# First layer of a four-stage decoder kernel: the input norm's scale is applied behind the projections instead of ahead of them

## The chip, the cores and the metric

One program runs on one core of a Trainium2 chip. The metric is device time in microseconds of one execution, from inputs in HBM to the output in HBM, as the median of several runs. Everything is in float32; products are made of parts, since a 32-bit value is split into a high part that TensorE takes in its fast 32-bit format and a low part with what is left.

TensorE (PE) multiplies, VectorE (DVE), ScalarE (ACT) and GpSimd (POOL) work on rows, SyncE (SP) issues most DMAs. Each engine runs its own list of instructions in order; semaphores connect them.

## The reference

The reference runs three blocks with 256 tokens of width 1024; only the first layer of the first block is touched. In it:

```python
def rmsnorm(x, g):
    xf = x.astype(jnp.float32)
    y = xf * lax.rsqrt(jnp.mean(xf * xf, axis=-1, keepdims=True) + EPS)
    return (y * g.astype(jnp.float32)).astype(x.dtype)

hn = rmsnorm(x, even_norm[i])
proj = hn @ even_w_in[i]
q, k, v, u = jnp.split(proj, [SWA_WIDTH, SWA_WIDTH + KV_WIDTH, SWA_WIDTH + 2 * KV_WIDTH], axis=-1)
q = rmsnorm(q.reshape(b, l, SWA_Q_HEADS, HEAD_DIM), q_norm[i])
k = rmsnorm(k.reshape(b, l, SWA_KV_HEADS, HEAD_DIM), k_norm[i])
v = v.reshape(b, l, SWA_KV_HEADS, HEAD_DIM)
o_attn = swa_sink_attention(q, k, v, sinks[i])
o_ssm = s5_mixer(u, ssm_a_re[i], ssm_a_im[i], ...)
mixed = jnp.concatenate([o_attn, o_ssm], axis=-1) @ even_w_out[i]
```

A factor that belongs to a token can be applied to `x` or, since the product is linear, to `proj`. For q and k a second norm per head follows, `q * rsqrt(mean(q*q) + EPS)`: with unscaled products q' and the token's scale s it is `q' * s * rsqrt(s*s*mean(q'*q') + EPS)`. `s5_mixer` is a state space model: it takes exponentials, sines and cosines of small parameter tables (a few instructions on 128x16 values), builds powers and matrices from them on DVE, and scans over the tokens.

## The kernel before

**Strips.** Every weight matrix is cut into strips of 128x1024 values, listed in the order of use (`strip_names`): in the first layer ("even") k, q0 to q3, v, u0 to u3 are strips 0 to 9, then follow parts of the output matrix and of the gate. A ring of three buffers holds them. SP issues strip n when strip n - 3 has its low part (`low_ready`, L499 and L500). ACT makes the high part (`high(n)`, L1254, which also waits until PE has done strip n - 3), DVE (`low(n)` in its own list, L1762) or POOL (`low(n)`, L2620) the low part. `high_to(n)` makes all high parts up to n that are still to be made.

**The first norm** (i = 0). ACT squares and sums each half of the tokens and takes the root (L1290, L1291), DVE inverts it and writes a diagonal matrix with the scales (`scale_diag`, L1807, L1808), PE multiplies x by this diagonal, which turns x and scales it (L687), and ACT (`parts`, L1280) and DVE (`parts`, L1798) write the high and the low part of `hT`, the normed and turned input, from PSUM. Between the roots and its `parts`, ACT makes high(0), two exponentials and two sines of the state space tables (L1303 to L1308); DVE makes low(0) and `decay_angles` (L1826 to L1844), which the sines wait for in the middle. POOL clears four areas, waits for the diagonals, and clears a fifth, `e_X` (L2632).

In the later layers the norm is taken differently (`SCALED_OUT` = [1, 2, 3]): x is turned as it is (`turn_x`, L665), PE spreads the scales over all rows (`widen_scale`, L673), DVE copies them to `scale_row` (`take_scale`, L1820), and the products are multiplied by it.

**The products of the layer.** `proj_fm` (L601) takes one strip: 16 products with the high part of the weights (L547 and L548), eight with the low part (L551). PSUM banks 4 and 5 take turns; product m waits until m - 1 earlier ones are evacuated (`evac`, L598). On ACT `out_and_square` evacuates k and the q's twice, as value and as square; `out_of` evacuates v, and `out_u` the u's. The squares are summed per head by PE (`head_sums`), ACT takes the root (L1381), DVE the reciprocal (`invert`, L1852), PE spreads it (`head_spread`) and DVE multiplies (`head_norm`, L1858).

**DVE's list** in this layer is written out by hand: low parts of the strips stand between pieces of the state space's preparation (powers and matrices of 128x768 values, `turns` which double tables of cosines and sines), then `head_norm`, `scores_in(0)` (L1975) and the softmax, then the scan for four groups (`ssm`), the sums (`y`) and the gate. Names of the form `low(5)` in this text mean the place in this list.

## Time and profile before

| what | value |
| --- | --- |
| runs | 1584.01, 1581.0, 1586.63 us; median 1584.01 us |
| profiled execution | 1583.31 us |
| its span | 1581.5 us |
| TensorE busy | 1541.3 us, 97% of the span |
| VectorE busy | 1197.7 us, 76% |
| ScalarE busy | 862.7 us, 55% |
| GpSimd busy | 249.0 us, 16% |
| chain that ended last, by engine | PE 88%, DVE 3%, ACT 2% |

The page lists busy times over the whole span. The first layer is its first 122 us; the rest of the kernel is the same before and after. Times in the rows below count from the start of the span. A row of the timeline is: start, duration, engine, line, operation, output and input with their shapes, count; behind it in brackets the idle time of the engine before it and what ended it.

### The profile page before, as it was taken

How to read it: one execution, taken by the hardware profiler on the slowest of the kernel's cores; microseconds unless marked ns; L12 is line 12 of the kernel's file. 1: busy time of each engine (PE TensorE's matmuls, PEld its weight loads, DVE VectorE, ACT ScalarE, POOL GpSimd, SP SyncE). 2: the span in 40 equal slices, each digit the busy share in tenths (PEclk: the TensorE clock that was granted, in tenths of full speed). 3: DMA queues.
4: the chain of work that ended last, by engine and by line, in shares of the span. 5: the costliest groups of instructions: out<-in, count | busy, mean ns of one | idle time of the engine just before them, and what ended most of it. 6: DMA issues, size and time to landing. Idle time of an engine off the chain costs nothing.

```text
span 1581.5 us, 30836 instructions
## 1 busy us (share of the span) xinstructions
PE 1541.3 (97%) x10491; PEld 1357.1 (86%) x10491; DVE 1197.7 (76%) x2328; ACT 862.7 (55%) x1319; POOL 249.0 (16%) x104
## 2 busy tenths in 40 slices
PE   7889999999999999999999999999999999999999
PEld 6878888888888887898899999988888888878887
DVE  7988888836688887666599852499999999975555
ACT  7765444568754444755556566455555444445553
POOL 2001000135100001000468746500000000000000
PEclk9899999999999999999999999999999999999999
DMA  6125556543465554433545565555554555555554
GB/s 223 59 95 182 184 192 189 183 147 120 149 207 191 189 195 147 147 108 107 172 148 187 173 185 176 193 171 168 169 172 161 175 173 178 172 177 190 195 190 155
DMA packets 72556, 264.65 MB, mean 167 GB/s; under 512 B 8080, under 2 KB 8336, under 8 KB 72112
## 3 DMA queue, kind: packets, MB, share of 16 engines
q1 hardware_dynamic: 71744, 261.00, 50.3%
q10 hardware_dynamic: 752, 2.83, 0.5%
q8 instruction: 40, 0.66, 0.2%
q14 instruction: 20, 0.16, 0.0%
HBM read 262.75 MB, written 1.05 MB: 167 GB/s over the span
## 4 chain that ended last, share of the span: by engine, by line
PE 88%; DVE 3%; ACT 2%; issue 1%; ACTq 0%; DVEq 0%
PE ps L695 33%; PE ps L558 17%; PE ps L562 9%; PE ps L547 7%; PE ps L548 6%; PE ps L551 6%; PE ps L1163 2%; PE ps L611 1%; DVE arena L1762 1%; PE ps L649 1%; PE ps L657 0%; PE ps L651 0%; PE ps L1125 0%; PE ps L979 0%; ACT w_hi L1254 0%
## 5 line engine op out<-in xcount | busy, mean ns | idle before, releaser
L1254 ACT ACTIVATE w_hi<-ring 128x1024 fp32r<-128x1024 f32 x489 | 515.6, 1057 | 338.5 <-PE ps L695 207.9
L1762 DVE TENSOR_TENSOR w_lo<-ring,w_hi 128x1024 fp32r<-128x1024 f32 x394 | 479.9, 1219 | 96.8 <-ACT w_hi L1254 82.8
L2620 POOL TENSOR_TENSOR w_lo<-ring,w_hi 128x1024 fp32r<-128x1024 f32 x95 | 240.4, 2541 | 759.3 <-ACT w_hi L1254 378.4
L558 PE MATMUL ps<-hT,w_hi 128*128 128x512 f32 x1184 | 298.5, 394 | 1.3 <-ACT w_hi L1254 1.3
L695 PE MATMUL ps<-w_hi,halves_hi 128*128 128x512 f32 x688 | 271.5, 395 | 0.6 <-DVE halves_lo L1762 0.6
L695 PE MATMUL ps<-w_hi,halves_lo 128*128 128x512 f32 x688 | 268.7, 391 | 0.0
L547 PE MATMUL ps<-hT,w_hi 128*128 128x256 f32 x984 | 250.5, 291 | 5.1 <-DVE hT L1798 3.2
L558 PEld LDWEIGHTS ps<-hT,w_hi 128*128 128x128 f32 x1184 | 215.0, 188 | 42.0 <-ACT w_hi L1254 1.7
L548 PE MATMUL ps<-hT,w_hi 128*128 128x256 f32 x984 | 245.2, 285 | 0.0
L547 PEld LDWEIGHTS ps<-hT,w_hi 128*128 128x128 f32 x984 | 190.7, 194 | 10.1 <-issue 6.9
L548 PEld LDWEIGHTS ps<-hT,w_hi 128*128 128x128 f32 x984 | 191.1, 194 | 0.1
L695 PE MATMUL ps<-w_lo,halves_hi 128*128 128x512 f32 x688 | 185.4, 390 | 0.0
L562 PEld LDWEIGHTS ps<-hT,w_lo 128*128 128x128 f32 x1184 | 161.4, 190 | 12.2 <-DVE w_lo L1762 0.7
L562 PE MATMUL ps<-hT,w_lo 128*128 128x256 f32 x1184 | 165.1, 282 | 0.0
L695 PEld LDWEIGHTS ps<-w_lo,halves_hi 128*128 128x128 f32 x688 | 129.0, 188 | 27.9 <-DVE w_lo L1762 0.6
L695 PEld LDWEIGHTS ps<-w_hi,halves_hi 128*128 128x128 f32 x688 | 129.4, 188 | 25.8 <-ACT w_hi L1254 1.4
L695 PEld LDWEIGHTS ps<-w_hi,halves_lo 128*128 128x128 f32 x688 | 129.5, 188 | 24.8
L1762 DVE TENSOR_TENSOR arena<-arena 128x256 f32<-128x256 f32 (+8 forms) x311 | 142.4, 480 | 9.6 <-ACT arena L1449 2.2
L1762 DVE TENSOR_TENSOR halves_lo<-arena,halves_hi 128x256 fp32r<-128x256 f32 (+1 forms) x180 | 82.2, 456 | 86.3 <-ACT halves_hi L1732 84.5
L551 PE MATMUL ps<-hT,w_lo 128*128 128x256 f32 x984 | 139.4, 285 | 0.0
L551 PEld LDWEIGHTS ps<-hT,w_lo 128*128 128x128 f32 x984 | 128.5, 194 | 0.0
L1762 DVE TENSOR_TENSOR arena<-ps,scale_diag 128x512 f32<-128x512 f32 (+2 forms) x120 | 74.0, 617 | 40.3 <-PE ps L562 40.1
(309 smaller groups left out, 1552.9 us busy)
## 6 DMA issues: line engine op xcount, KB each, us to landing
ring<-in_strips SPq DMA_DIRECT2D x489, 512.0 KB, 3.4
const<-in_const SPq DMA_DIRECT2D x1, 1352.0 KB, 11.9
x_s<-in_x SPq DMA_DIRECT2D x2, 512.0 KB, 4.6
arena<-in_rel ACTq DMA_DIRECT2D x1, 1024.0 KB, 4.7
arena<-in_keys ACTq DMA_DIRECT2D x1, 1024.0 KB, 6.2
out<-x_s SPq DMA_DIRECT2D x4, 256.0 KB, 2.2
arena<-in_ssm_bc SPq DMA_DIRECT2D x1, 512.0 KB, 6.8
arena<-in_ssm_b SPq DMA_DIRECT2D x1, 512.0 KB, 8.1
```

The costliest lines, as they stand in the source:

```text
L547: pe.matmul(out, w[0][:, cols], hT_hi[:, c, :], start=c == 0, stop=False)
L548: pe.matmul(out, w[0][:, cols], hT_lo[:, c, :], start=False, stop=False)
L551: mm = pe.matmul(out, w[1][:, c * P:(c + 1) * P], hT_hi[:, c, :], start=False, stop=c == KC - 1)
L558: pe.matmul(bank, w[0][:, c * P:(c + 1) * P], hT[:, c].rearrange("p s t -> p (s t)"), start=c == 0, stop=False, skip_group_check=True)
L562: mm = pe.matmul(bank[:, 0:T], w[1][:, c * P:(c + 1) * P], hT_hi[:, c, :], start=False, stop=c == KC - 1, skip_group_check=True)
L611: return pe.matmul(ps[:, VALUE_BANKS[2 * a + b], :], x[:, j, a * P:(a + 1) * P], w[part][:, 512 * b:512 * b + 512], start=j == 0 and x is ...
L649: pe.matmul(o, hT_hi[:, 4 * half + c, tok], w[0][:, cols], start=half == 0 and a == 0 and c == 0, stop=False, skip_group_check=True)
L695: return pe.matmul(ps[:, 2 * a + b, :], x[:, a * P:(a + 1) * P], w[part][:, b * 512:(b + 1) * 512], start=first and part == 0 and x is hi, ...
L1163: mm = pe.matmul(ps[:, 6 + g % 2, q * HALF:(q + 1) * HALF], oh_second[:, g % 3, q * P:(q + 1) * P], oh_gate[:, g % 3, (2 * q + part) * HAL ...
L1254: sc.activation(w_hi[:, n % RING, :], ring[:, n % RING, :], ACT.Copy).then_inc(high_ready, 1)
L1762: return ve.tensor_tensor(o, a, b, op)
L2620: po.tensor_tensor(w_lo[:, n % RING, :], ring[:, n % RING, :], w_hi[:, n % RING, :].bitcast(F32), ALU.subtract).then_inc(low_ready, 1)
```

## The change

The first norm joins the later ones in `SCALED_OUT`. What it does, engine by engine:

- **PE** turns x by transposes as soon as it has landed, without scales. Behind `head_sums` it spreads the scales (`widen_scale(0)`, bank 6). `in_matrices` waits for `scale_ready`.
- **ACT**: the first table is that of the exponential. The order is now: exponential of log_dt, high(0), second exponential, `parts`, high(1), the sines, high(2). The squares and roots of x stand behind the evacuation of q1 and ahead of that of q2. The root of the head sums has its scaling done by DVE. v is written with the scale of its tokens, in two instructions where it was one. The u's are no longer evacuated by ACT; only their place in the order of the high parts stays (`u_split`).
- **DVE**: `decay_angles` comes first and is cut in two; `parts` stands ahead of the second half (`decay_sines`). low(0) is gone; low(2) stands behind the wait for the sines. New in the list: `scales(0)` between low(5) and the next product, `take_scale(0)` and `scale_squares` behind low(6), `u_out(0)` to `u_out(3)` behind low(7), low(8), low(9) and `turns(8)`, and one more multiplication in `invert`.
- **POOL** clears `e_X` without waiting for the diagonals, and then makes low(0).
- `strip_two` and `proj_two` are defined but called nowhere.

```diff
-SCALED_OUT = [1, 2, 3]
-SCALE_BANK = {1: 2, 2: 5, 3: 2}
+SCALED_OUT = [0, 1, 2, 3]
+SCALE_BANK = {0: 6, 1: 2, 2: 5, 3: 2}
```

In PE's list:

```diff
+                if i == 0:
+                    small_wait(pe, "first")
+                    for a in range(NT):
+                        small_wait(pe, "x%d" % a)
+                        for c in range(KC):
+                            mm = pe.transpose(norm_at(0, c)[:, a * P:(a + 1) * P], x_s[:, a, c * P:(c + 1) * P],
+                                              ident)
+                            if a == NT - 1:
+                                mm.then_inc(turned, 1)
+                    return
...
+                    pe.wait_ge(scale_ready, 1)
...
                 head_sums(e_sq, 5, 1)
+                widen_scale(0)
                 proj_fm(("even", "u", 0))
```

In ACT's list:

```diff
+            def root(i, a):
+
+                ch.link(sc.activation(xn[:, a, :], x_s[:, a, :], ACT.Square, accum_out=stat[:, a:a + 1]))
+                sc.activation(stat[:, 2 + a:3 + a], stat[:, a:a + 1], ACT.Sqrt, bias=k("eps"),
+                              scale=1.0 / D).then_inc(roots, 1)
+
-                ch.add(sc.activation(stat[:, 6:7], k("eps"), ACT.Sqrt))
+                ch.add(sc.activation(stat[:, 6:7], k("eps"), ACT.Sqrt if i else ACT.Exp))
...
+                if i == 0:
+                    small_wait(sc, "param")
+                    sc.activation(e_p[:, 0, :], prm("log_dt"), ACT.Exp).then_inc(prm_act, 1)
+                    high_to(0)
+                    sc.wait_ge(prm_dve, 1)
+                    sc.activation(e_p[:, 3, :], e_p[:, 1, :], ACT.Exp).then_inc(prm_act, 1)
+                    parts()
+                    high_to(1)
+                    sc.wait_ge(prm_dve, 2)
+                    sc.activation(e_p[:, 9, :], e_p[:, 6, :], ACT.Sin).then_inc(prm_act, 1)
+                    sc.activation(e_p[:, 10, :], e_p[:, 7, :], ACT.Sin).then_inc(prm_act, 1)
+                    high_to(RING - 1)
+                    return
...
-                def out_u(j):
-                    out_of(("even", "u", j), e_u[:, j],
-                           lambda b: ps[:, b, 0:T].rearrange("p (b s) -> p s b", s=LC))
+                def u_split(j):
+                    high_to(AT[("even", "u", j)] + RING - 1)
+                    nproj[0] += 1
...
                 out_and_square(("even", "k", 0), 4)
-                for j in range(3):
+                for j in range(2):
                     out_and_square(("even", "q", j), j)
+                for a in range(NT):
+                    small_wait(sc, "x%d" % a)
+                    root(0, a)
+                out_and_square(("even", "q", 2), 2)
...
-                sc.wait_ge(sq_summed, 1)
-                sc.activation(e_rt[0:16, 0, :], ps[0:16, 1, 0:T], ACT.Sqrt, bias=k("eps")[0:16],
-                              scale=1.0 / HD).then_inc(rt_ready, 1)
-                out_u(0)
+                sc.wait_ge(sq_scaled, 1)
+                sc.activation(e_rt[0:16, 0, :], e_rt[0:16, 0, :], ACT.Sqrt,
+                              bias=k("eps")[0:16]).then_inc(rt_ready, 1)
+                u_split(0)
```

In DVE's list:

```diff
+                if i == 0:
+                    small_wait(ve, "param")
+                    decay_angles()
+                    parts()
+                    decay_sines()
+                    return
...
-            def invert(n, rows):
+            def invert(n, rows, scaled=False):
 
                 ve.wait_ge(rt_ready, n)
-                ve.reciprocal(rows, rows).then_inc(rs_ready, 1)
+                ins = ve.reciprocal(rows, rows)
+                if scaled:
+                    ch.link(ins)
+                    ins = tt(rows, rows, scale_row[0:16], ALU.mult)
+                ins.then_inc(rs_ready, 1)
+
+            def scale_squares(n, rows, bank):
+
+                ve.wait_ge(sq_summed, n)
+                ch.link(tt(rows, ps[0:16, bank, 0:T], scale_row[0:16], ALU.mult))
+                ve.scalar_tensor_tensor(out=rows, in0=rows, scalar=1.0 / HD, in1=scale_row[0:16], op0=ALU.mult,
+                                        op1=ALU.mult).then_inc(sq_scaled, 1)
...
             def even():
-                for n in range(1, RING):
-                    low(n)
+                ve.wait_ge(low_ready, 1)
+                low(1)
                 small_wait(ve, "ssm")
                 ve.wait_ge(prm_act, 4)
+                low(2)
...
+                def u_out(j):
+
+                    ve.wait_ge(strip_done, AT[("even", "u", j)] + 1)
+                    ve.wait_ge(evac, 6 + j)
+                    m = 6 + j
+                    by_step = lambda a: a.rearrange("p (b s) -> p s b", s=LC)
+                    tt(e_u[:, j], by_step(ps[:, 4 + m % 2, 0:T]), by_step(scale_row), ALU.mult).then_inc(evac, 1)
...
                 low(5)
+                small_wait(ve, "first")
+                scales(0)
...
                 low(6)
+                take_scale(0)
+                scale_squares(1, e_rt[0:16, 0, :], 1)
...
                 low(7)
-                invert(1, e_rt[0:16, 0, :])
+                u_out(0)
+                invert(1, e_rt[0:16, 0, :], True)
...
                 low(8)
+                u_out(1)
...
                 low(9)
+                u_out(2)
                 turns(4)
...
                 turns(8)
+                u_out(3)
```

In POOL's list:

```diff
-            po.wait_ge(diag_ready, NT)
             po.memset(e_X[:, :, :, :, :], 0.0).then_inc(zeroed, 1)
+            low(0)
```

## Rows read from the trace of the kernel before

**Rows 1.** Waits of the first 120 us: us, times, longest us

```profile
PE ps L687 <- DVE scale_diag L1808: 7.3, 1, 7.3
PE ps L820 <- ACT arena L1424: 5.3, 1, 5.3
```

**Rows 2.** Stretches: length, busy us of PE, PEld, DVE, ACT, POOL, clock, DMA

```profile
35.00:45.00 10.00, 10.00 (x76) 8.49 (x76) 9.86 (x12) 8.33 (x13) 0.00 (x0) 1.00 0.33 107
```

**Rows 3.** Chain of waits at the layer's end: start us, us, what

```profile
105.75 1.13 DVE w_lo L1762
...
107.28 0.39 PE ps L528
```

**Rows 4.** Timeline of ACT and DVE at 67 and 78 us

```profile
67.42 2.88 ACT L1405 ACTIVATE xn<-xn,arena 128x128 f32<-128x128 f32 x8 [0.53 <-DVE arena L1995]
...
77.94 0.17 DVE L1762 TENSOR_TENSOR arena<-arena 128x8 f32<-128x8 f32 x1 [0.57 <-ACT arena L1362]
```

**Rows 5.** Timeline of ACT at the start

```profile
5.13 1.04 ACT L1290 ACTIVATE xn<-x_s 128x1024 f32<-128x1024 f32 x1
...
7.86 1.04 ACT L1254 ACTIVATE w_hi<-ring 128x1024 fp32r<-128x1024 f32 x1
...
8.92 1.28 ACT L1303 ACT_TABLE_LOAD   x1
```

**Rows 6.** Timeline of DVE at the start

```profile
10.82 1.25 DVE L1831 TENSOR_SCALAR arena<-arena 128x16 f32<-128x16 f32 x1
...
12.95 0.17 DVE L1836 TENSOR_SCALAR arena<-arena 128x16 f32<-128x16 f32 x1
...
14.94 3.23 DVE L1798 SCALAR_TENSOR_TENSOR hT<-ps,param,hT 128x256 fp32r<-128x256 f32 x8 [0.46 <-ACT hT L1280]
```

**Rows 7.** Timeline of POOL, and DVE beside a halving on POOL

```profile
2.06 3.52 POOL L2628 MEMSET arena<- 128x4096 f32 x1
...
8.53 3.51 POOL L2632 MEMSET arena<- 128x4096 f32 x1 [2.85 <-DVE scale_diag L1808]
...
356.88 5.42 POOL L2620 TENSOR_TENSOR w_lo<-ring,w_hi 128x1024 fp32r<-128x1024 f32 x2 [2.32 <-ACT w_hi L1254]
...
357.35 2.70 DVE L1762 TENSOR_TENSOR halves_lo<-arena,halves_hi 128x768 fp32r<-128x768 f32 x1
```

**Rows 8.** Timeline of DVE: low(3), low(5) and scores_in(0)

```profile
22.43 1.23 DVE L1762 TENSOR_TENSOR w_lo<-ring,w_hi 128x1024 fp32r<-128x1024 f32 x1 [1.73 <-ACT w_hi L1254]
...
30.50 1.22 DVE L1762 TENSOR_TENSOR w_lo<-ring,w_hi 128x1024 fp32r<-128x1024 f32 x1
...
57.30 1.95 DVE L1975 SCALAR_TENSOR_TENSOR xn<-ps,const 128x384 f32<-128x384 f32 x4
```

**Rows 9.** Timeline of PE's first strips, and a stretch as in rows 2

```profile
15.57 0.36 PE L547 MATMUL ps<-hT,w_hi 128*128 128x256 f32 x1 [2.76 <-DVE hT L1798]
...
18.85 1.91 PE L551 MATMUL ps<-hT,w_lo 128*128 128x256 f32 x8
...
22.70 1.12 PE L551 MATMUL ps<-hT,w_lo 128*128 128x256 f32 x8
...
25.58 1.13 PE L551 MATMUL ps<-hT,w_lo 128*128 128x256 f32 x8
...
17.50:21.00 3.50, 3.50 (x18) 3.44 (x18) 3.20 (x7) 1.70 (x3) 0.00 (x0) 0.52 0.12 26
```

**Rows 10.** Timeline of DVE: a diagonal, a reciprocal, five operations out of PSUM

```profile
8.19 0.29 DVE L1808 TENSOR_SCALAR scale_diag<-const,stat 128x128 f32<-128x128 f32 x1
...
41.75 1.73 DVE L1852 RECIPROCAL arena<-arena 16x256 f32<-16x256 f32 x1
...
53.34 2.05 DVE L1858 SCALAR_TENSOR_TENSOR arena<-arena,param,ps 128x256 f32<-128x256 f32 x5
```

**Rows 11.** DMAs: what, count, KB, us to landing; strip 3, issued at 10.34

```profile
param<-in_param ACTq DMA_DIRECT2D x1, 76.0 KB, 5.3
...
DMA to landing us min/median/max: 7.7/7.7/7.7
```

89 lines of the change are left out of this document (49 added, 40 removed).

## The prediction

> **What bounds the kernel now.** The page comes first: PE is busy for 97% of the span, and its chain of waits is PE nearly throughout, so a change of the first layer can only pay where PE is not yet the bound. The waits of PE in the first 120 us are the second view. They show 7.3 us until the first product, which is what the change attacks, and 5.3 us of standing still at 74 us for a copy of ACT [rows 1]. So PE does not set the pace inside this layer. The busy times by stretch, third, name who does: DVE works 9.86 us of ten between 35 and 45 [rows 2], and the stretches on both sides of it look alike. The chain of waits, fourth, ends for this layer in DVE's halving of strips (L1762) and passes to PE only at 107.28, where the gated product waits for DVE [rows 3]. The timeline shows where DVE's queue hands over on the way: at 67.42 ACT waits for DVE, at 77.94 DVE waits 0.57 us for ACT, whose work from 67.42 had no gap [rows 4]. From low(3) at 22.43 to scores_in(0) at 57.30 no row of DVE's timeline names an idle time ahead of it but the first of them [rows 8].
>
> From this I take one rule for the whole account: **the layer ends later or earlier by as much as DVE reaches scores_in(0) later or earlier** (57.30 before). Behind it DVE, ACT and PE follow from each other without slack, and from 107 us PE is full in unchanged work. The question is whether the earlier start is worth more than what is put into DVE's queue.
>
> **The start.** Before, DVE begins the low parts of hT at 14.94 [rows 6], and PE its first strip at 15.57 [rows 9]. After, neither the squares nor the scales stand ahead of the turned x. ACT waits for param (the second DMA of its queue, issued at 1.2, 5.3 us to its landing [rows 11], so at 6.5), takes its exponential, high(0) from about 7.8 to 8.9 (it begins at 7.86 before [rows 5]), the second exponential, and from 9.0 on its eight parts, ahead of DVE's. DVE can begin its angles at 6.8 and is ready for L1831 at 7.1. But POOL no longer waits for the diagonals before it clears e_X: this memset now follows the one that ends at 5.6, and lasts from 5.65 to 9.15 [rows 7]. The row of L1831 tells what that means: this 128x16 TENSOR_SCALAR took 1.25 us, until 12.07, and the memset on POOL ended at 12.04 [rows 6, 7], where the same operation takes 0.17 at 12.95 [rows 6]. So L1831 stands until 9.15. Then low(0), new on POOL, has its input since 8.9 and starts at once. A halving on POOL is 2.4 us (two in 5.42, of which 0.7 were lost to DVE), and the DVE operation that met it took 2.70 us [rows 7]. L1832 needs L1831's result first, so I take it that POOL gets in between and DVE stands until 11.6. The rest of the angles costs 0.65 us (12.07 to 12.95 is four steps with one more wait [rows 6]). DVE's parts then begin at 12.25 in place of 14.94: **2.7 us gained**. Bounds of this step: 5.0 us gained (no second stop: 9.9), and 2.4 (L1831 itself waits for both).
>
> The rows leave open whether the small operations of DVE could slip through while POOL halves: the one that met a halving has two inputs in SBUF, L1832 has one. The Trainium skill, SBUF — State Buffer, section "Who interferes with whom", says that whichever instruction starts first holds the pair of ports shared by VectorE and GpSimd for its whole length, that `tensor_scalar` can need the pair, and that two inputs in SBUF collide only with a GpSimd instruction that reads SBUF. The trace agrees where it shows something: L1831 stopped for a memset, the two-input products just ahead of it did not. By that rule L1832 waits for all of low(0), 2.7 us gained; if only two-input operations met it, L1834 would, with the same end.
>
> **From there to low(3).** DVE: parts 3.2 us, to 15.5; the sines, which stood at 12.95 to 14.5 (14.94 less 0.46 of idle time [rows 6]), 1.5 us, to 17.0; low(1) and low(2) at 1.14 each (low(3) at 22.43 is 1.14 ahead of the next instruction), to 19.3; three small ones, to 19.6. ACT's sines and high(2) run from 16.4 to 17.7 and cost nothing: DVE is busy then. PE: its last pair of the first strip follows DVE's last part, the eight low products follow it. Before these took 1.91 us, at 18.85, since the granted clock was at 1.2 GHz there (0.52 as the mean of 17.5 to 21); at 2.4 GHz they take 1.12 [rows 9]. I assume the low clock again, since PE stands still for 4 us ahead of this strip (2.8 before): first strip done at 17.6. Evacuating k is 0.55, high(3) 1.05: ready at 19.3, and its strip, issued after low(0), lands at about 18.0, as before (10.34 + 7.7 [rows 11], behind the same queue of constants). low(3) starts at 19.6, 2.8 us ahead of 22.43. PE is 2.9 us ahead as well.
>
> **From low(3) to low(5): the squares in ACT's queue.** DVE needs 8.07 us from low(3) to low(5) (22.43 to 30.50 [rows 8]) and would be there at 27.7. But the two roots now stand between q1 and q2 on ACT, and behind them in the queue is high(5), for which low(5) waits. PE takes 2.88 us for a strip (22.70 to 25.58 [rows 9]), so the third is done at 17.6 + 5.8 = 23.4; evacuated at 23.95; the roots cost 2.73 us (5.13 to 7.86) and one table load of 1.28 [rows 5], since the sines' table is in: 27.95; high(5) until 29.0. **DVE stands for 1.3 us**, and low(5) starts at 29.05, 1.45 us ahead of before. Bounds of the stop: nothing if PE is 1.3 us earlier, 2.8 if PE has one more stretch at 1.2 GHz. PE waits as well, for the evacuation of q2 ahead of v, but DVE's work is longer there. The load of Sqrt at 38.9 goes away; ACT has slack there and it pays nothing.
>
> The Trainium skill, ScalarE: Activation LUTs, section "What ACT_TABLE_LOAD costs", puts a switch at about 2.66 us, load and drain together. Here the row of the load at 8.92 is 1.28 us and the next activation starts at 10.21; the measurement decides. By the page the stop would be 1.4 us longer, the sum 1587.9.
>
> **What is added to DVE**, all between low(5) and scores_in(0), with no idle time to take it up:
> - scales(0): twice a reciprocal, 0.2, and a diagonal, 0.2 to 0.29 (8.19 [rows 10]): 0.82 us. Before, this lay where DVE waited anyway.
> - take_scale: one 128x256 out of PSUM with a wait on itself: 0.46. Five such operations take 2.05 us [rows 10].
> - scale_squares: two of 256 columns, the first waited for: 0.80.
> - u_out: four of 128x256 out of PSUM, 0.35 to 0.41 each: 1.5. They stood on ACT. The strided reading (every fourth column) has no row on DVE; I take it as free, at most twice: 3.0.
> - invert: one more of 256 columns behind the reciprocal of 1.73 [rows 10]: 0.44.
>
> Sum **4.0 us**, between 3.5 and 5.5. PE's widen_scale (four passes, 0.5 us) is due at 36.3 on DVE and done at 35.4; the wait of u2 and u3 for DVE's evacuations ends 2 to 5 us before PE comes, since PE waits for low(7) and low(8) anyway. ACT loses four evacuations and is idle longer before the scores' exponentials: no gain, as DVE's maxima are later. Transposes instead of 128-column products save PE about 2 us in a stretch where DVE is late: no gain.
>
> **Sum.** 4.0 - 1.45 = **+2.55 us**. The profiled execution took 1583.31 (span 1581.5), 0.7 under the median of 1584.01 and inside the runs' 1581.0 to 1586.6: it would be 1585.9 with a span of 1584.0. The median: **1586.5**.
>
> **Rivals.**
> - *A, DVE slips past POOL at 9.2.* For: L1832 could be queued in time. Against: it waits for L1831 by semaphore. Parts from 9.9, PE 2.3 us earlier, but high(3) now waits for its strip at 18.0 and low(3) starts at 19.1: 3.3 us gained. The roots are done at 25.6 and the stop at low(5) vanishes: 4.0 - 3.3 = +0.7, 1584.7.
> - *B, DVE is not the bound.* Then the additions are free and the start's gain arrives: 1584.0 - 2.8 = 1581.2. For: PE's wait of 7.3 us is the largest. Against: rows 2 to 4.
> - *C, the low clock lasts, the side beyond 0.3%.* Because DVE now stops at low(5) for ACT, and ACT for PE's third strip, every microsecond that PE loses before 23.4 goes through. The stretch of before, 17.5 to 21, cost about 1.5 us (16 products at a distance of 0.21 where 28 would fit at 0.12, which is what 1.91 and 1.12 us for eight come to [rows 9]). One more gives 1588.0, two more 1589.5, slower by over 0.3%; it decides from 1.5 such stretches on. For: PE is idle longer and fed slowly from 12.8 to 16. Against: the stretch of before ended at 21, when PE was full.
> - *D, the strided u_out costs double:* 1588.0.
>
> **Chances.** Forecast 0.50; A 0.20; B 0.05; C with one stretch or D 0.15; C with two, or C and D together, 0.10. A measurement of this kernel can tell about 0.3%, 4.75 us, from no change: faster than 1579.3 would need B and more, 0.03; slower than 1588.8 is the last case and a tail of the one before it, 0.13; the rest 0.84. The range takes in A on one side (less the scatter of a median) and one more stretch or D on the other: 1582.5 to 1589.0.
>
> **What would show it.** L1831 on DVE long, until about 9.15, and L1832 about 2.3 us long beside low(0) on POOL; DVE's first part at 12.25; low(3) at 19.6; an idle time of DVE before low(5) that ends on ACT's w_hi, 1.3 us; scores_in(0) at 59.8; PE's first gated product at 109.8. Wrong if DVE stops somewhere else for longer, if L1832 isn't stopped, or if the layer ends before 107 although DVE reaches the scores later: then DVE was not the bound.

## The result and the profile after

The changed kernel takes 1584.74 us (median of 20 runs, 1581.70 to 1597.42), the kernel before 1582.26 us (median of 20, 1579.16 to 1586.63). The ratio is 1.0025 with a 95% interval of [1.0014, 1.0037], which is 2.2 to 5.9 us more. The middle of the interval is within 0.3%, and the whole interval lies above 1: the change made the kernel slower, by little. The profiled execution of after took 1582.71 us, with a span of 1580.9: less than the 1583.31 and 1581.5 of before. So the two profiles taken alone say the opposite of the medians, and why they do is the first lesson. The stretch from 660 to 700 us holds the same work in both kernels:

The stretch of before, and then of after; the columns are as in rows 2.

```profile
660.00:700.00 40.00, 39.97 (x262) 34.98 (x262) 29.46 (x52) 18.47 (x36) 0.00 (x0) 0.91 0.34 110
```

```profile
660.00:700.00 40.00, 39.97 (x288) 35.49 (x287) 31.37 (x54) 20.82 (x40) 0.00 (x0) 1.00 0.36 119
```

TensorE is busy throughout in both, but its granted clock was 0.91 of full speed in the one and 1.00 in the other: the same 40 us did 9% less work. The first product of the next layer (mlp0) starts 3.1 us later in after, that offset is still 3.1 at 662 us, and at 687 us it is 0.1: this stretch takes it away again. It says nothing about the change. Only the first layer can be compared between the two profiles, so I read it mark by mark.

**The start.** PE's waits of the first 120 us of after, in the columns of rows 1:

```profile
PE ps L709 <- DMA const<-in_const: 5.1, 1, 5.1
PE ps L855 <- ACT arena L1472: 4.2, 1, 4.2
PE ps L548 <- DVE hT L1844: 3.9, 1, 3.9
PE ps L791 <- DVE arena L1927: 2.9, 1, 2.9
```

The wait of 7.3 us [rows 1] is gone, but PE waits 3.9 us for DVE's parts after its transposes and, new, 2.9 us ahead of the attention (L791). POOL and DVE show what held the parts up.

Timeline of POOL, then of DVE, in after (columns as in rows 4):

```profile
5.59 3.51 POOL L2717 MEMSET arena<- 128x4096 f32 x1
9.15 2.34 POOL L2706 TENSOR_TENSOR w_lo<-ring,w_hi 128x1024 fp32r<-128x1024 f32 x1
```

```profile
7.31 1.83 DVE L1884 TENSOR_SCALAR arena<-arena 128x16 f32<-128x16 f32 x1
9.17 2.35 DVE L1885 TENSOR_SCALAR arena<-arena 128x16 f32<-128x16 f32 x1
11.55 0.17 DVE L1886 TENSOR_SCALAR arena<-arena 128x16 f32<-128x16 f32 x1
...
12.06 3.22 DVE L1844 SCALAR_TENSOR_TENSOR hT<-ps,param,hT 128x256 fp32r<-128x256 f32 x8
```

The clearing of e_X ends at 9.10, and L1884 (L1831 before [rows 6]) stood with it until 9.14. low(0) on POOL ends at 11.49, and L1885 stood with it until 11.52. The same operation takes 0.17 us at 11.55. The parts start at 12.06 in place of 14.94 [rows 6].

**From low(3) to scores_in(0)**, timeline of DVE in after, to be compared with rows 8:

```profile
19.20 1.23 DVE L1810 TENSOR_TENSOR w_lo<-ring,w_hi 128x1024 fp32r<-128x1024 f32 x1
...
28.97 1.23 DVE L1810 TENSOR_TENSOR w_lo<-ring,w_hi 128x1024 fp32r<-128x1024 f32 x1 [1.51 <-ACT w_hi L1290]
...
36.28 0.42 DVE L1873 COPY scale_diag<-ps 128x256 f32<-128x256 f32 x1
...
42.25 0.59 DVE L1810 TENSOR_TENSOR arena<-ps,scale_diag 128x256 f32<-128x256 f32 x1
...
60.38 1.95 DVE L2059 SCALAR_TENSOR_TENSOR xn<-ps,const 128x384 f32<-128x384 f32 x4
```

And what DVE's stop of 1.51 us is made of, timeline of ACT in after:

```profile
23.86 1.06 ACT L1305 ACTIVATE xn<-x_s 128x1024 f32<-128x1024 f32 x1
...
25.03 1.28 ACT L1306 ACT_TABLE_LOAD   x1
26.33 0.30 ACT L1306 ACTIVATE stat<-stat,const 128x1 f32<-128x1 f32 x1
...
27.90 1.04 ACT L1290 ACTIVATE w_hi<-ring 128x1024 fp32r<-128x1024 f32 x1
```

low(3) is 3.23 us early, low(5) is 1.53 us early, because ACT squares x and takes roots for 4.0 us ahead of high(5), and scores_in(0) is 3.08 us late, because of what DVE does in between. One difference between the two profiles is not the change's. In before, PE's first strip ran in part at the low clock [rows 9]; in after the granted clock was 1.00 throughout:

```profile
17.00:21.00 4.00, 4.00 (x36) 4.00 (x35) 3.99 (x14) 2.54 (x6) 0.00 (x0) 1.00 0.47 146
```

What that is worth is worked out behind the experiments.

**The end of the layer.** The chain of waits in after has the first gated product at 109.66, for 107.28 [rows 3]: 2.38 us later. The lines before it are DVE's, as they were.

```profile
108.13 1.14 DVE w_lo L1810
109.27 0.35 DVE hT L1810
109.61 0.04 issue
109.66 0.39 PE ps L529
```

At the handover to mlp0 another 0.7 us is lost (first product at 127.94, for 124.85). PE waits there for ACT, which had waited for a strip to land. This is the strip's high part, on ACT in after:

```profile
125.01 1.06 ACT L1290 ACTIVATE w_hi<-ring 128x1024 fp32r<-128x1024 f32 x1 [2.24 <-DMA ring<-in_strips]
```

The same wait is 1.64 us in before. So the profiled execution of after is 3.1 us late when the changed part ends.

### The profile page after: what moved, and what is told of

It is laid out like the page before. It is cut to its first block, busy times and chain, and to the rows that moved or that the text cites. A ratio compares the mean times of both kernels' runs of the same rounds, so it can differ in the third digit from the quotient of the medians.

```text
span 1580.9 us, 30822 instructions
## 1 busy us (share of the span) xinstructions
PE 1537.4 (97%) x10479; PEld 1352.3 (86%) x10479; DVE 1202.5 (76%) x2335; ACT 860.0 (54%) x1315; POOL 251.5 (16%) x105
## 4 chain that ended last, share of the span: by engine, by line
PE 86%; DVE 3%; ACT 2%; issue 1%; DMA 1%; ACTq 0%; DVEq 0%; SPq 0%
PE ps L729 31%; PE ps L579 17%; PE ps L583 9%; PE ps L548 7%; PE ps L549 6%; PE ps L552 6%; PE ps L1199 2%; PE ps L637 1%; DMA ring<-in_strips 1%; DVE w_lo L1810 1%; DVE arena L1810 1%; ACT w_hi L1290 1%; PE ps L675 1%; PE ps L677 0%; PE ps L683 0%
## 5 line engine op out<-in xcount | busy, mean ns | idle before, releaser
L1290 ACT ACTIVATE w_hi<-ring 128x1024 fp32r<-128x1024 f32 x489 | 515.7, 1057 | 346.7 <-PE ps L729 206.7
L1810 DVE TENSOR_TENSOR arena<-ps,scale_diag 128x512 f32<-128x512 f32 (+3 forms) x125 | 76.8, 615 | 40.6 <-PE ps L583 40.5
```

Source lines behind the costliest of these rows:

```text
L1290: sc.activation(w_hi[:, n % RING, :], ring[:, n % RING, :], ACT.Copy).then_inc(high_ready, 1)
L1810: return ve.tensor_tensor(o, a, b, op)
```

## The experiments

I had two questions. Is DVE's queue the account that sets the layer's end (my theory), or does something else take the place of what was removed? And why do the runs differ by 3.8 us on average (1586.04 against 1582.27 us) when the marks differ by 2.4 to 3.1? Three theories stood for the second: the offset at mlp0 grows in other runs; a part of the changed code costs more than its row says; or TensorE's clock is lower in the changed kernel. Each experiment is one edit of one of the two kernels. The marks that I quote for each are the start of low(5), of scores_in(0) and of the first gated product in its profile.

### e1: POOL out of DVE's way

In the changed kernel, low(0) comes first on POOL and the clearing of e_X waits until the angles are done.

```diff
-            po.memset(e_X[:, :, :, :, :], 0.0).then_inc(zeroed, 1)
             low(0)
+            po.wait_ge(prm_dve, 2)
+            po.memset(e_X[:, :, :, :, :], 0.0).then_inc(zeroed, 1)
```

> The changed kernel with one thing changed on GpSimd: low(0) comes first, and the clearing of e_X waits until the angles are done. Theory (L1884 and L1885 stood 1.83 and 2.35 us because GpSimd held the shared port pair): both take 0.17 us, VectorE's first part of hT begins at about 9.1 where it was 12.06, but low(3) is held by its strip's landing at about 18 and starts at 19.1 at best (19.20 in the changed kernel), so scores_in(0) gains at most 1.5 us (the stop before low(5), if PE's third strip is done earlier): 59 us where it was 60.38. Rival (the small operations were slow for another reason): they stay at about 2 us, first part at 12. In total: 0 to 1.5 us less than the changed kernel.

Measured: ratio 1.0021 [1.0003, 1.0038]. Timeline of DVE in e1:

```profile
7.27 0.17 DVE L1884 TENSOR_SCALAR arena<-arena 128x16 f32<-128x16 f32 x1
7.48 0.17 DVE L1885 TENSOR_SCALAR arena<-arena 128x16 f32<-128x16 f32 x1
...
9.66 3.23 DVE L1844 SCALAR_TENSOR_TENSOR hT<-ps,param,hT 128x256 fp32r<-128x256 f32 x8 [1.38 <-ACT hT L1322]
...
19.07 1.23 DVE L1810 TENSOR_TENSOR w_lo<-ring,w_hi 128x1024 fp32r<-128x1024 f32 x1 [2.10 <-ACT w_hi L1290]
...
27.14 1.22 DVE L1810 TENSOR_TENSOR w_lo<-ring,w_hi 128x1024 fp32r<-128x1024 f32 x1
```

Both stops are gone, 1.83 and 2.35 us become 0.17 and 0.17, and the parts start 2.4 us sooner. This shows that POOL's two instructions caused them. Of the 2.4 us, low(3) sees 0.13, since it now waits 2.10 us for a high part whose strip has just landed; but ACT and PE are so far ahead that the stop at low(5) is gone, and scores_in(0) is at 58.60, 1.78 ahead of after. Those are the steps of my rival A: it said 19.1 for low(3) and 3.3 us gained over before, and low(5) at 27.14 is 3.36 us ahead of 30.50 [rows 8] (2.3 ahead of e5 below, which is the kernel before up to there, without the low clock in its first strip).

The layer's end did not follow. The first gated product is at 113.70, 4 us later than in after. Timeline of PE in e1:

```profile
62.53 13.93 PE L820 MATMUL ps<-arena 32*128 32x64 f32 x256
```

These are the 256 small products of `block_in`. They take 7.39 us in after and 7.37 in before. Here they ran at the low clock (granted clock 0.50, so 1.2 GHz) and took 13.93 us, and both ACT and DVE waited behind them. This was the first sign of an answer to the second question.

### e2: the squares leave the critical queue

In the changed kernel, ACT squares x in its idle time ahead of the sines; only the roots stay between q1 and q2.

```diff
                     high_to(1)
+                    for a in range(NT):
+                        small_wait(sc, "x%d" % a)
+                        ch.add(sc.activation(xn[:, a, :], x_s[:, a, :], ACT.Square, accum_out=stat[:, a:a + 1]))
                     sc.wait_ge(prm_dve, 2)
...
+                ch.wait()
                 for a in range(NT):
-                    small_wait(sc, "x%d" % a)
-                    root(0, a)
+                    sc.activation(stat[:, 2 + a:3 + a], stat[:, a:a + 1], ACT.Sqrt, bias=k("eps"),
+                                  scale=1.0 / D).then_inc(roots, 1)
```

> The changed kernel with the two squares of x moved to ScalarE's idle time ahead of the sines; only the two roots and the table load stay behind q1. Theory (VectorE's stop of 1.51 us before low(5) is the squares in ScalarE's queue): the stop is gone, low(5) starts at 27.5 instead of 28.97, and as nothing behind it has slack scores_in(0) and the end of the layer come 1.5 us earlier. Rival (the stop is only moved, to take_scale or low(6)): the layer's end stays within 0.5 us of the changed kernel's.

Measured: ratio 1.0039 [1.0025, 1.0054] with a median of 1588.38 us over 7 runs: not better than after, if anything worse. Timeline of DVE in e2:

```profile
27.90 1.22 DVE L1814 TENSOR_TENSOR w_lo<-ring,w_hi 128x1024 fp32r<-128x1024 f32 x1
...
35.67 0.42 DVE L1877 COPY scale_diag<-ps 128x256 f32<-128x256 f32 x1 [0.38 <-PE ps L699]
```

low(5) has no stop ahead of it and starts 1.07 us sooner, although the first strip ran at the low clock in this profile and low(3) was 0.62 later (19.82). So the squares in ACT's 4.0 us in front of high(5) made the stop of 1.51. Half of that gain goes at `take_scale`, where DVE has overtaken PE and waits 0.38 us for the widened scale. scores_in(0) is at 59.79 (-0.59), the first gated product at 109.05 (-0.61). In this profile the layer is shorter, the runs are not: 4 of the 7 had a mean granted clock of 0.986 to 0.988.

### e3: u back on ACT

In the changed kernel, ACT takes the four u out of PSUM as it did before. The multiplication of u by its tokens' scale is left out, so the output is wrong and only the times count.

```diff
                 def u_split(j):
-                    high_to(AT[("even", "u", j)] + RING - 1)
-                    nproj[0] += 1
+                    out_of(("even", "u", j), e_u[:, j],
+                           lambda b: ps[:, b, 0:T].rearrange("p (b s) -> p s b", s=LC))
...
-                u_out(0)
-                u_out(1)
-                u_out(2)
-                u_out(3)
```

> The changed kernel with the four u strips evacuated by ScalarE as before; the multiplication of u by the token's scale is left out, so this part of the computation is missing. Theory (VectorE sets the layer's pace; four evacuations with a strided read hold it for 0.51 to 0.57 us each): scores_in(0) 2.1 us earlier, at 58.3, and the layer's end too. Rival (VectorE has slack, ScalarE or TensorE is the bound): the layer's end does not move.

Measured: ratio 1.0017 [1.0002, 1.0032]. low(5) started at 29.91, 0.94 later than in after, since PE's first strips ran longer at the low clock in this profile, and the stop there was 1.92 us. scores_in(0) was at 59.25. From low(5) to scores_in(0) that is 29.34 us, for 31.41 in after: the four u_out cost DVE 2.07 us. The first gated product was at 108.88.

### e4, e11, e12: the order alone

In the kernel before, only the order changes: ACT's and DVE's parts ahead of the sines, low(2) behind a wait, e_X cleared after the angles. The norm stays where it was and nothing is added to DVE.

```diff
                     sc.activation(e_p[:, 3, :], e_p[:, 1, :], ACT.Exp).then_inc(prm_act, 1)
+                    parts()
+                    high_to(1)
                     sc.wait_ge(prm_dve, 2)
...
                     parts()
+                if i == 0:
+                    decay_sines()
...
-            po.wait_ge(diag_ready, NT)
+            po.wait_ge(prm_dve, 2)
             po.memset(e_X[:, :, :, :, :], 0.0).then_inc(zeroed, 1)
```

> The kernel before with the order of the changed one alone: x is still scaled by the diagonal, but ScalarE's and VectorE's parts of hT come ahead of the sines, low(2) comes behind the wait for the sines, and GpSimd clears e_X after the angles. Nothing is added to VectorE's queue. Theory: the first part begins at 12.0 instead of 14.94, everything behind it shifts by 2.5 to 3 us, the layer ends at 104.5 (first gated product behind y(3), 107.28 before) and the kernel takes 2.5 to 3 us less than before (ratio 0.998). Rival (the early start is taken back by a later wait, for a strip's landing or ScalarE): less than 1 us.

Measured: ratio 0.9987 [0.9974, 1.0000]. DVE's parts start at 12.88, 2.06 us sooner than before, and scores_in(0) at 55.28 is 2.02 us sooner, so the gain reaches it whole. But the first gated product is only 0.53 us sooner, at 106.75. Timelines of PE and of DVE in e4 show where the rest went:

```profile
81.36 2.82 PE L859 MATMUL ps<-const,arena 128*128 128x128 f32 x12 [1.90 <-ACT arena L1407]
```

```profile
87.06 0.76 DVE L1764 TENSOR_TENSOR hT<-ps,hT 128x256 fp32r<-128x256 f32 x2 [1.80 <-ACT hT L1435]
```

The twelve products that turn the second four heads' probabilities took 1.53 us in before and 2.82 here, at the low clock, and DVE then waited 1.80 us for ACT behind them, for 0.35 before. Whether DVE sooner is always taken back like this, or only where the clock is low, e8 below tells.

I ran two more of this form. e11 is the same without the last edit (e_X cleared early, as before):

> The kernel before with the order alone, as in the experiment e4, but with e_X cleared as early as in the kernel before, behind the diagonals. If the stop of DVE's angle for that clearing (1.25 us before) matters, DVE's parts start about 1 us later than in e4 (12.88), and scores_in(0) is at 56.2 or so; if ACT's parts limit them anyway (DVE waited 1.01 for ACT in e4), the parts start at 12.9 and scores_in(0) stays at 55.3. Median as e4's or up to 1 us more.

Measured: ratio 1.0007 [0.9995, 1.0019]. The angle L1835 (L1831 in before) again took 1.24 us beside the clearing, the parts started at 12.85, scores_in(0) was at 55.16: the second case of what was expected: the stop was hidden behind ACT's parts. e12 is e4 once more, unchanged:

> The kernel of e4 once more: the kernel before with the order alone. Its ratio was 0.9987 [0.9974, 1.0000]. If the layer's earlier end (0.5 us) and a granted clock slightly above that of before are both real, the ratio comes out at 0.998 to 1.000 again; if e4's clock was luck, at 0.9997 or above.

Measured: ratio 1.0001 [0.9990, 1.0012]. Its layer ended at 106.15, 1.13 us sooner than before. With e4 and e11 the three ratios are 0.9987, 1.0007 and 1.0001: the order alone makes no difference that these runs can tell, and e4's better ratio did not come again. All three lie below the 1.0025 of after, which has the same order and the scale behind the projections besides: that, with the work that it adds, made the kernel slower, and not the order.

### e5: DVE later in the kernel before

In the kernel before, DVE does three 128x768 operations that nothing needs (2.94 us) ahead of scores_in(0), and nothing else changes. This is the plainest test of my rule.

```diff
                 turns(8)
+                for _ in range(3):
+                    ch.link(tt(e_tmp[:, 1, :], e_tmp[:, 1, :], e_tmp[:, 1, :], ALU.mult))
                 small_wait(ve, "const")
```

> The kernel before with three operations of 128x768 on VectorE's scratch area ahead of scores_in(0), 0.92 us each, 2.8 us in all, that nothing needs. Theory (VectorE's arrival at scores_in(0) sets the layer's end): the first gated product behind y(3) comes at 110.0 instead of 107.28, and the lowest of the runs rises by 2.7 us. Rival (slack behind the scores): under 1 us. Beside that, if TensorE's standing still ahead of the scores makes the low clock fall more often on the 256 small products behind them, the mean granted clock of the runs falls under the 0.994 of the kernel before, and the runs spread upwards.

Measured: ratio 1.0053 [1.0034, 1.0073]; five of six runs took 1589.9 to 1592.4 us, and one 1584.5. scores_in(0) was at 59.23 (+1.93, since DVE was 1.07 us ahead at low(5) in this profile), but the first gated product was at 115.36: **8.1 us later for a DVE 1.9 us later**. Timeline of PE in e5:

```profile
59.84 1.04 PE L757 MATMUL ps<-arena 64*128 64x128 f32 x3 [3.77 <-DVE xn L1975]
...
63.16 13.93 PE L785 MATMUL ps<-arena 32*128 32x64 f32 x256
```

PE stood still for 3.77 us inside the attention, its clock fell to 0.50, and `block_in` ran at it from end to end. From scores_in(0) to the gated product that is 56.1 us, for 50.0 in before: 6 us for the low clock, on top of the delay. What the delay costs while the clock stays up rests on one run: the one at 1584.5 had a mean clock of 0.994 and is 1.3 us above the mean of the kernel before. None of my rivals was this one; C comes nearest, a loss of PE at the low clock that is passed on.

The edit stands behind low(5), so up to there e5 is a second profile of the kernel before, and it lacks the low clock in PE's first strip. Timeline of DVE in e5, for 30.50 in [rows 8]:

```profile
29.43 1.22 DVE L1762 TENSOR_TENSOR w_lo<-ring,w_hi 128x1024 fp32r<-128x1024 f32 x1
```

### e6: both repairs together

e1 and e2 in one kernel.

> Both e1_port and e2_squares on the changed kernel. low(3) stays at 19.1 since its strip's landing holds it, low(5) at 27.1, so the layer's end is that of e1_port where its clock is high: by VectorE 58.6 for scores_in(0), 1.8 us ahead of the changed kernel. What VectorE needs for the added work remains: lowest of the runs about 1581, 2 us over the kernel before. If the squares' place made a difference of its own, it would be below 58.3.

Measured: ratio 1.0016 [0.9999, 1.0032]. low(5) at 27.24, scores_in(0) at 58.68, first gated product at 108.17: 1.5 us sooner than in after, 0.9 later than before. The two repairs together give what e1 gives alone (58.60), since both remove the same stop at low(5). With the gated product at 108.17, the additions to DVE still leave the layer later than it was.

### e7 and e8: does work on PE keep the clock up?

PE stands still for 2.88 us ahead of the attention in after. e7 puts 22 products there whose result nobody reads.

```diff
                 proj_fm(("even", "u", 3))
+                for c in range(22):
+                    pe.matmul(ps[:, 0, 0:T], hT_hi[:, c % KC, 0:P], hT_hi[:, c % KC, :], start=True, stop=True)
                 attention(0, e_qk, EVEN_HEADS)
```

> The changed kernel with 22 products of 256 columns that nothing reads, on TensorE where it stands 2.88 us ahead of the scores. Theory (the changed kernel's runs above 1585 come from the low clock over the 256 small products, brought on by TensorE standing still): the mean granted clock rises from 0.991 to 0.994 or more, the runs above 1588 go, the median falls by 1.5 to 2.5 us; scores_in(0) stays at 60.4. Rival (the spread has another source, anywhere in the kernel): median and clock stay as they are.

Measured: ratio 1.0032 [1.0015, 1.0048], scores_in(0) at 61.40, first gated product at 112.71. In the profile the attention and `block_in` ran at full clock (7.37 us), but the second turn of the probabilities ran at the low one (2.82 us). The mean clock of the runs did not rise (0.9912, for 0.9913 in after), and two of nine runs were at 0.987. The expectation that filled idle time would bring the clock back, and with it the median, failed.

The products stand ahead of the attention, so up to there e7 is a second profile of after, and in it the first strip ran at the low clock. The stretch to 21 us, and low(5) in the timeline of DVE:

```profile
17.00:21.00 4.00, 4.00 (x29) 4.00 (x29) 3.37 (x7) 1.99 (x4) 0.00 (x0) 0.77 0.47 170
```

```profile
29.95 1.23 DVE L1812 TENSOR_TENSOR w_lo<-ring,w_hi 128x1024 fp32r<-128x1024 f32 x1 [1.96 <-ACT w_hi L1292]
```

e8 puts 8 products ahead of the attention and 30 ahead of `y_local(0)` into e4.

```diff
                 proj_fm(("even", "u", 3))
+                for c in range(8):
+                    pe.matmul(ps[:, 0, 0:T], hT_hi[:, c % KC, 0:P], hT_hi[:, c % KC, :], start=True, stop=True)
                 attention(0, e_qk, EVEN_HEADS)
...
                 lag_matrices()
+                for c in range(30):
+                    pe.matmul(ps[:, 3, 0:T], hT_hi[:, c % KC, 0:P], hT_hi[:, c % KC, :], start=True, stop=True)
                 y_local(0)
```

> e4_order_only with 8 such products ahead of the scores and 30 behind the lag matrices, where TensorE stood 5.3 us. Theory (e4 lost 1.5 of its 2.0 us behind the scores because the second turn of probabilities ran at the low clock, 2.82 us instead of 1.53, and VectorE waited 1.80 us): the layer's end moves from 106.75 to 105.3, the ratio to before is 0.998 or lower. Rival (the loss sits in ScalarE's queue): end at 106.7 as before.

Measured: ratio 0.9998 [0.9984, 1.0011]. Timeline of PE in e8:

```profile
66.17 3.86 PE L904 MATMUL ps<-hT 128*128 128x256 f32 x30
...
71.50 1.73 PE L820 MATMUL ps<-arena 128*128 128x192 f32 x12 [1.48 <-ACT arena L1430]
73.07 1.48 PE L859 MATMUL ps<-const,xn 128*128 128x128 f32 x12
```

y_local took 1.73 us for 3.22 in before (PE's wait ahead of it, 5.3 us in [rows 1], is filled to 1.48), and scores_in(0) at 54.55 and the first gated product at 104.95 are 2.75 and 2.33 us sooner than before. So in the profile the filler did what it was for at y_local. The second turn of the probabilities still took 2.82 us there, as in e4; what came back is PE's time ahead of it, and nearly all of DVE's gain reached the layer's end. So DVE sooner is not taken back by itself. The median, again, shows nothing of it.

### e9 and e10: what makes u_out dear

u_out reads two tensors at every fourth column: u in PSUM, and the row of scales in SBUF. e9 reads both in their own order, e10 only the scales; u then stands in the wrong order or has the wrong scales, and only the times count.

```diff
-                    tt(e_u[:, j], by_step(ps[:, 4 + m % 2, 0:T]), by_step(scale_row), ALU.mult).then_inc(evac, 1)
+                    tt(e_u[:, j].rearrange("p s b -> p (s b)"), ps[:, 4 + m % 2, 0:T], scale_row, ALU.mult).then_inc(evac, 1)
```

```diff
-                    tt(e_u[:, j], by_step(ps[:, 4 + m % 2, 0:T]), by_step(scale_row), ALU.mult).then_inc(evac, 1)
+                    tt(e_u[:, j], by_step(ps[:, 4 + m % 2, 0:T]), scale_row.rearrange("p (s b) -> p s b", s=LC), ALU.mult).then_inc(evac, 1)
```

> The changed kernel, with u taken out of PSUM column by column in its own order, the scale row read in its own order too (u then stands in another order: what follows computes with wrong columns). In the changed kernel the four u_out took 0.59 to 0.61 us, with 0.51 to 0.57 to the next instruction. Theory S, the reading at every fourth column is what costs: each takes 0.41 to 0.42 us like take_scale (0.42), and scores_in(0) starts some 0.6 us earlier, at about 59.8. Theory T, a product with a second tensor costs that, whatever its order: 0.60 stays and so does 60.4. The median moves by less than can be told either way.

> The changed kernel, where only the scale row is read in its own order and u in PSUM still at every fourth column (the product has wrong scales). If the strided operand in PSUM carries the cost, the four u_out stay at 0.60 us; if the strided operand in SBUF does, they take 0.41; if each adds half, 0.50.

Measured: ratios 1.0029 [1.0015, 1.0043] and 1.0025 [1.0010, 1.0040]. Timeline of DVE, first e9, then e10:

```profile
42.52 0.42 DVE L1810 TENSOR_TENSOR arena<-ps,scale_diag 128x256 f32<-128x256 f32 x1
...
59.91 1.94 DVE L2059 SCALAR_TENSOR_TENSOR xn<-ps,const 128x384 f32<-128x384 f32 x4
```

```profile
48.09 0.42 DVE L1810 TENSOR_TENSOR arena<-ps,scale_diag 128x256 f32<-128x256 f32 x1
```

0.42 us in both, for 0.59 to 0.61 in after. The strided reading in PSUM costs nothing, the strided reading in SBUF costs the whole 0.18 us of each. Four of them make 0.7 us: from low(5) to scores_in(0) e9 takes 30.66 us, for 31.41. The Trainium skill, SBUF — State Buffer, section "Specifications (TRN2)", gives SBUF lines of 16 bytes of which at least two reads must hit each for full speed; every fourth column of 4 bytes is a new line each time, and the row agrees with that. It gives 8-byte lines for PSUM, but e10 shows no cost of the same step there for DVE.

Both profiles show more than they were made for. These are the stretches of e9, and behind them those of after:

```profile
60.00:64.00 4.00, 3.86 (x22) 2.78 (x22) 3.90 (x8) 0.00 (x0) 0.00 (x0) 0.50 0.01 4
64.00:72.00 8.00, 8.00 (x155) 8.00 (x156) 7.69 (x25) 5.69 (x23) 0.00 (x0) 0.50 0.01 3
```

```profile
60.00:64.00 4.00, 4.00 (x23) 2.97 (x19) 3.97 (x7) 0.00 (x0) 0.00 (x0) 0.50 0.00 0
64.00:72.00 8.00, 8.00 (x276) 7.63 (x279) 7.62 (x26) 5.21 (x22) 0.00 (x0) 0.98 0.02 5
```

The two kernels do the same work on PE there. In both, the clock is at its low level (0.50) from 60 us on, in the attention products, which come right after PE's idle time of 2.7 and 2.9 us. In after's profile it is back when `block_in` begins at 64.31 (0.98); in e9's it stays, `block_in` takes 13.93 us, and the first gated product is at 116.05, 6.4 us later than after's although DVE reached the scores 0.5 us sooner. That execution took 1591.75 us.

### What the runs of all kernels say together

**The low clock in many runs.** How often does that happen? The mean granted clock that comes with every run gives a hint: it was 0.986 and 0.986 in the profiled executions of e9 and e10, 0.988 and 0.989 in those of e1 and e5, the four with `block_in` at 13.93 us, and 0.991 to 0.996 in all others.

| kernels | runs | of them at a clock of 0.988 or less |
| --- | --- | --- |
| before (three comparisons), e4, e8, e11, e12 | 134 | 0 |
| after, e1, e2, e3, e6, e7, e9, e10 | 90 | 20, at 1587.8 to 1597.4 us |
| e5 (before with DVE later) | 6 | 4, at 1590.5 to 1592.4 us |

The mark of 0.988 was chosen after the runs, and it is no sharp one: e5's profiled execution lies just above it, and so do six of the 89 runs of before (0.989, 1586.8 to 1587.4 us). With 0.990 as the mark the counts are 20 of 134, 30 of 90 and 5 of 6. The mean clock doesn't say where in the kernel the clock was low either; only the profiled executions do.

After itself had 3 such runs of 20; without them its mean is 1584.50 us, 2.2 us above the 1582.27 of the kernel before. So of the 3.8 us between the means, 2.2 us are in the ordinary executions, near the 2.4 us of the account of DVE's queue, and 1.5 us come from three executions with the low clock. Two of these (1595.05 and 1597.42 us) are over 10 us above the mean of the others, more than `block_in` at the low clock costs in any profile, and no profile shows what else was slow in them.

**The start, at like clocks.** PE's first strip ran at the low clock, wholly or in part, in the profiles of before, e2, e3 and e7, and at full clock in those of after, e5, e9 and e10. So the 1.53 us gained at low(5) compare unlike executions. Both at the low clock (e7 and e3 against before) low(5) is at 29.95 and 29.91 for 30.50; both at full clock (after and e9 against e5) at 28.97 and 29.25 for 29.43. The change gains 0.2 to 0.6 us at low(5), and with the 4.6 us that it adds behind it scores_in(0) comes some 4.1 us later: 61.40 in e7, for 57.30. The other microsecond of the 1.53 was the luck of this pair of profiles. How often either kernel starts at which clock no run tells, so the 4.1 us can't be set against the 2.5 us of the medians; that gap stays open. The same holds for e4, e11 and e12, whose first strip ran at full clock: their scores_in(0) is 2.0 to 2.4 us sooner than in the profile of before, but by an estimate from e5's low(5) (29.43 + 26.80 = 56.23) only 0.9 to 1.3 sooner at like clocks.

**From the scores to the layer's end.** In the ten profiles with `block_in` at full clock, y_local starts 16.93 to 16.96 us after scores_in(0), even in after, whose attention ran 1.1 us longer at the low clock. In most of them the last 22.0 us, from `values_mixed` to the gated product, are the same too. What differs in between is the clock of PE's small products. y_local and both turns of the probabilities can each run at either level; from the scores to the gated product it is 49.3 us at least (after, e2) and 51.5 at most (e4, e11), with 50.0 in before. PE's rows of y_local, before and after, show 0.7 us of it:

```profile
74.24 3.22 PE L820 MATMUL ps<-arena 128*128 128x192 f32 x12 [5.26 <-ACT arena L1424]
```

```profile
77.31 2.54 PE L855 MATMUL ps<-arena 128*128 128x192 f32 x12 [4.16 <-ACT arena L1472]
```

So DVE's arrival at the scores does set the layer's end, in both directions, with 0.7 us less to 1.5 us more for the clock behind it; with `block_in` at the low clock the way to the end is 55.1 to 56.2 us.

## Why the prediction was right

The forecast was 1586.5 in a range of 1582.5 to 1589.0, with "within 0.3%" at 0.84. The median is 1584.74, and the difference to the kernel before is +2.5 by the medians for +2.5 forecast. The prediction stood on the first median of before, 1584.01, which 20 runs put at 1582.26; that is why the sum lies 1.8 us above the result while the difference meets it. That the two differences agree to a tenth is luck in good part, as the points show: the median of after contains executions with the low clock, and in the profiles a start that came out 1 us too well stands against the costs.

- **The rule** (the layer ends as much later as DVE reaches scores_in(0)): right for after, 3.08 us in, 2.38 out, and for e8 in the other direction, 2.75 in, 2.33 out. "Behind it DVE, ACT and PE follow from each other without slack" left out that PE's clock differs from execution to execution there: 49.3 to 51.5 us with `block_in` at full clock, over 55 without. That is why e4 gave back 0.5 of 2.0 us and e5 made 8.1 of 1.9.
- **POOL's two instructions stop DVE**: as forecast. L1831 (L1884 after) until 9.14 for 9.15, L1832 (L1885) 2.35 us long for 2.4, parts at 12.06 for 12.25. The rule of the Trainium skill (SBUF — State Buffer, section "Who interferes with whom"), that an instruction holds the shared pair for its whole length, agrees: a `tensor_scalar` with one input in SBUF waited out all of low(0), and e1 removed both waits by moving POOL's work. Rival A (DVE slips past) fell. Made real in e1, it gave 3.36 us at low(5) for 3.3 against this profile of before, and 2.3 at like clocks.
- **low(3)** at 19.20 for 19.6: 0.4 us better, 0.2 from the parts and 0.2 from DVE's operations behind them. The low clock that I had assumed for the first strip was not there in this profile: its eight low products took 1.29 us for the 1.91 assumed. In e2, e3 and e7 it was there, they took 1.91, and low(3) started at 19.82 to 19.84, behind ACT's high part.
- **The stop at low(5)**: 1.51 us for 1.3, low(5) at 28.97 for 29.05, and this closeness is luck. The forecast assumed the low clock, and with it the stop was 1.92 and 1.96 us and low(5) at 29.91 and 29.95 (e3, e7): the sum had the first strip done 0.6 us too soon, since its high products run longer at that clock too. ACT's row has 4.0 us of squares, roots and one table load, as summed; e2 removed the stop by moving the squares. The load's row is 1.28 us and the next activation started 0.02 us behind it, so the 2.66 us that the Trainium skill, ScalarE: Activation LUTs, section "What ACT_TABLE_LOAD costs", gives for load and drain don't appear as time lost here.
- **The additions to DVE**: 4.0 forecast, 4.6 measured (31.41 less 26.80 us from low(5) to scores_in(0); e7, with the low clock in the first strip, has 31.45). The mis-sized term is u_out, taken as 1.5 with the strided reading free: it measured 2.07 (e3). e9 and e10 put 0.7 of it to the strided read of the scales in SBUF, which I had not even named; I had thought of PSUM. Rival D was the right doubt at less than half its price (0.6 of 1.5 us); without the strided read the additions would have been 3.9.
- **scores_in(0)** at 60.38 for 59.8, and **the first gated product** at 109.66 for 109.8. The second is closer because 0.7 us came back behind the scores: y_local took 2.54 us for 3.22, since the low clock ended sooner in it. That is luck of the execution.
- **The handover to mlp0** cost 0.7 us more in this profile, by a strip that landed late. The prediction had the layer's offset pass through unchanged. The two misses of 0.7 cancel.
- **Rival B** (DVE is not the bound) fell: e3 took 2.07 us from DVE, and the layer ended 0.8 us sooner even though DVE stopped longer at low(5).
- **Rival C** (the low clock lasts) named the right kind of loss. Where I looked for it, in PE's strips ahead of 23.4, it comes in some profiles (e2, e3, e7) and is worth 1 us at low(5). The dearer place is behind 58 us, and that one I had not seen. PE stands still ahead of the attention, which it never did between 25 and 62 us before. In five of the profiles with DVE later (after, e1, e5, e9, e10) the clock is low in the attention, and in the four of them where `block_in` runs at it too the layer loses 5 to 6 us. The prediction saw PE's cover shrink, "PE waits for low(7) and low(8) anyway", and counted it as free. That was the step left out. The range held it by its upper end, meant for something else.

What stays open is what lets the clock fall there and whether it outlasts the attention. Idle time of PE is not enough: e2 stood still for 2.88 and 1.30 us around the start of the attention and had the full clock there in its profile, e4 stood still for 2.2 us and never shows a run at 0.988, and e7 filled the idle time with products and neither the mean clock nor the share of low runs improved. It may not be needed either. In before the clock was low from 52 to 55 us, ahead of the attention, although PE had not stood still for over 30 us:

```profile
52.00:53.00 1.00, 1.00 (x6) 1.00 (x6) 0.97 (x8) 0.00 (x0) 0.00 (x0) 0.50 0.17 16
```

So runs with the low clock come more often with the kernels in which DVE is later; that PE's idle time ahead of the attention is the cause is not shown, and the count in the table is as far as these runs go.

## What to carry to other kernels

When work moves onto the engine that sets the pace, price every operand's reading, those in SBUF too, and look at which engine now stands still behind it: on TensorE a stretch of small products behind it can cost more by the low clock than the delay itself, and it may do so in only some of the executions. Compare the low-clock share of many runs and the marks inside the changed part, and don't compare two spans. Ahead of a comparison of marks, compare the granted clock of the stretches in front of them: here 1 us of a gain of 1.5 was the clock of one strip. An earlier start is worth only what reaches the next queue that is full: here 2.9 us at DVE's parts became 0.2 to 0.6 at low(5) at like clocks, and a loss at the scores.

## What the runs showed of the hardware that I had not expected

- A DVE operation of 128x256 with one operand in SBUF read at a step of 16 bytes took 0.60 us, with the same step in PSUM only 0.42, and without a step 0.42.
- 256 products of 32x64 took 7.37 us at 2.4 GHz and 13.93 at 1.2 GHz: the low clock costs them the factor 1.89.
- The same kernel can have a stretch at either clock: the first strip of the changed kernel ran at a granted clock of 1.00 in one profile and of 0.50 from 12 to 18 us in another (after, e7).
- An unchanged stretch of 40 us with TensorE busy throughout was granted 0.91 of its clock in one profile and 1.00 in another of the same length. Over the 89 runs of the kernel before, a mean granted clock lower by 0.001 went with 1.0 to 1.1 us more (slopes of 990, 1004 and 1057 us per unit in the three comparisons; those of the other kernels, from fewer runs, lie between 700 and 1330).
- A 128x16 operation of DVE that takes 0.17 us alone took 1.83 and then 2.35 us beside POOL, each time to within 0.04 us of the end of POOL's instruction.
